# Gate copies and outputs of a state space stage two pairs later, a small store moved to GpSimd, and group norm sums placed ahead of the last attention tile

## The reference, cut to what matters

```python
y_attn = diff_attention(q, k, v, ...) @ w_attn_branch
xbc = silu(causal_depthwise_conv(xbc, conv_w, conv_b))          # 24 chunks of 128 channels
dt  = softplus(dt_raw + dt_bias);  a = -exp(a_log)
cum = cumsum(dt * a)                                            # per head, along the tokens
w[t, s] = (C_t . B_s) * exp(cum_t - cum_s) * dt_s   for s <= t  # per head, 32 heads
y   = w @ x_head + d_skip * x_head
y   = y * silu(z);  y = rms_norm of each of 4 groups of 512 channels
y_ssd = y @ w_ssd_branch
mixed = (sigmoid(g_attn) * y_attn + sigmoid(g_ssd) * y_ssd) @ w_out
```

## Time and profile before

| what | us |
|---|---|
| median of 3 runs | 1904.21 (1900.37 to 1904.4) |
| the profiled execution, its own time | 1904.04 |
| its span, first to last instruction | 1902.4 |
| TensorE busy | 1691.4 (89%) |
| VectorE busy | 917.0 (48%) |
| ScalarE busy | 556.3 (29%) |
| GpSimd busy | 326.9 (17%) |
| mean granted clock of TensorE | 0.968 of full speed |

### The profile page before, as it was taken

How to read it: one execution, slowest core, us unless ns; L and a number is a source line. 1 busy time by engine, 2 the same in 40 slices (tenths; PEclk the granted TensorE clock), 3 DMA queues, 4 the chain that set the end, 5 groups by cost and what they waited for, 6 DMA issues and landing times.

```text
span 1902.4 us, 30539 instructions
## 1 busy us (share of the span) xinstructions
PE 1691.4 (89%) x12330; PEld 1587.1 (83%) x12330; DVE 917.0 (48%) x2286; ACT 556.3 (29%) x1511; POOL 326.9 (17%) x300
## 2 busy tenths in 40 slices
PE   5999989989999878777898799867699999999998
PEld 4788868778879878776898799867599999989998
DVE  5641373444146666776797765458743210231200
ACT  0111223660033444433457321224623110132100
POOL 0100000000003444444424221224500000020000
PEclk9998999999999999999999999988899999999999
DMA  8962348323439999999999999999967888755783
GB/s 363 373 233 91 128 117 224 109 92 129 155 105 403 407 420 421 421 421 419 421 412 412 418 420 420 420 391 397 353 240 248 329 291 298 253 194 192 275 292 132
DMA packets 85450, 563.15 MB, mean 296 GB/s; under 512 B 8832, under 2 KB 17600, under 8 KB 17984
## 3 DMA queue, kind: packets, MB, share of 16 engines
q0 software_dynamic: 39744, 289.42, 37.1%
q1 hardware_dynamic: 38992, 256.05, 36.4%
q10 hardware_dynamic: 6576, 15.76, 3.1%
HBM read 556.96 MB, written 4.23 MB: 295 GB/s over the span
## 4 chain that ended last, share of the span: by engine, by line
PE 67%; DMA 19%; DVE 6%; ACT 4%; issue 3%; ACTq 0%; SPq 0%; POOL 0%; DVEq 0%
PE PS L885 30%; PE PS L633 21%; DMA AUX<-in_peer_uv_dram,SCR 10%; PE PS L849 7%; DMA ring<-in_stream_dram 6%; DMA CONV<-in_peer_uv_dram,SCR 1%; DMA V<-in_peer_uv_dram,SCR 1%; PE PS L704 1%; DVE PROJ L2048 1%; PE PS L655 1%; PE PS L679 1%; PE PS L753 1%; ACT PROJ L1401 1%; ACT small L1393 0%; PE PS L978 0%
## 5 line engine op out<-in xcount | busy, mean ns | idle before, releaser
L633 PE MATMUL PS<-H,ring 128*128 128x256 f32 x1280 | 292.8, 391 | 7.8 <-DMA ring<-in_stream_dram 4.1
L633 PEld LDWEIGHTS PS<-H,ring 128*128 128x128 f32 x1280 | 249.5, 197 | 45.0 <-issue 9.7
L849 PE MATMUL PS<-PROJ,AUX 128*128 128x128 f32 x1632 | 204.1, 284 | 71.5 <-ACT PROJ L1401 71.1
L885 PE MATMUL PS<-H,ring 128*128 128x128 f32 x2272 | 262.0, 276 | 3.9 <-DMA ring<-in_stream_dram 2.1
L885 PEld LDWEIGHTS PS<-H,ring 128*128 128x128 f32 x2272 | 258.3, 193 | 5.1 <-issue 4.1
L849 PEld LDWEIGHTS PS<-PROJ,AUX 128*128 128x128 f32 x1632 | 193.5, 197 | 80.1 <-ACT PROJ L1401 80.0
L1204 POOL DMA_INDIRECT AUX<-in_peer_uv_dram,SCR x124 | 148.5, 1197 | 473.5 <-DVE SCR L2032 228.7
L849 PE MATMUL PS<-PROJ,CONV 128*128 128x128 f32 x1328 | 173.1, 293 | 50.8 <-ACT PROJ L1401 50.8
L849 PEld LDWEIGHTS PS<-PROJ,CONV 128*128 128x128 f32 x1328 | 166.4, 207 | 56.1 <-ACT PROJ L1401 55.7
L885 PE MATMUL PS<-PROJ,ring 128*128 128x128 f32 x1664 | 192.5, 276 | 9.6 <-DMA ring<-in_stream_dram 9.6
L885 PEld LDWEIGHTS PS<-PROJ,ring 128*128 128x128 f32 x1664 | 188.9, 192 | 11.7 <-DMA ring<-in_stream_dram 9.9
(11 more groups left out here) (337 smaller groups left out, 1948.9 us busy)
## 6 DMA issues: line engine op xcount, KB each, us to landing
ring<-in_stream_dram SPq DMA_DIRECT2D x185, 1024.0 KB
AUX<-in_stream_dram SPq DMA_DIRECT2D x51, 1024.0 KB, 4.9
AUX<-in_ada_dram POOLq DMA_DIRECT2D x16, 1024.0 KB, 9.9
PROJ<-in_ada_dram ACTq DMA_DIRECT2D x4, 1024.0 KB, 20.3
AUX<-in_ada_dram SPq DMA_DIRECT2D x4, 1024.0 KB, 19.9
bias_skewed<-AUX ACTq DMA_DIRECT2D x1, 3072.0 KB, 34.2
ring<-in_stream_dram ACTq DMA_DIRECT2D x2, 1024.0 KB
PROJ<-in_rgw_dram ACTq DMA_DIRECT2D x2, 1024.0 KB, 10.4
```

The lines of the kernel that those rows point to most:

```text
L633: mm = pe.matmul(acc(n, c), w[:, k, c * P:(c + 1) * P], src[:, g * DC + k, :], start=(g == 0 and k == 0 and (c == 0 or groups == 1)), stop ...
L849: mm = pe.matmul(y_chunk(t, c), UV[b][:, D + c * P:D + (c + 1) * P], DIAG[turn % ND], start=(k == 0 and c % 4 == 0), stop=(k == SPT - 1), ...
L885: mm = pe.matmul(acc2(u, n)[:, c * P:(c + 1) * P], w[:, k, c * P:(c + 1) * P], src, start=(g == 0 and k == 0 and (c == 0 or groups == 1)), ...
```

## The change

- ScalarE copies gate tile (h + 2)/4 behind segment h and decay h-1, for h = 6, 10, ..., 26, instead of tile 1 + h/4 ahead of segment h, for h = 4, 8, ..., 24.
- VectorE runs `gate_out` two pairs behind the weighing instead of one.
- The store of the cumulative sums is issued by GpSimd instead of ScalarE, with a semaphore of its own.
- TensorE makes the four group norm sums ahead of the fourth attention tile instead of behind it. VectorE's work is put in matching order: two groups' squares are added behind each of the first two attention outputs, and groups 0 and 1 are normed before the fourth attention output is taken, groups 2 and 3 after it.
- Two semaphores of ScalarE are merged into one (`early_exp`).

```diff
-            for t in range(4):
+            for t in range(3):
                 project("attn", t, YA)
             for g in range(GROUPS):
                 pe.wait_ge(S("squares_added"), g + 1)
                 sum_chunks(("gn", g), CONV[:, 4 * g:4 * g + 1, :], 1)
+            project("attn", 3, YA)
...
-            pool.wait_ge(S("rows_stored"), 32)
+            wait_taken(pool, "cumt")
+            pool.dma_start(cum_rows, CUMT).then_inc(S("cumt_stored"), 16)
+            pool.wait_ge(S("cumt_stored"), 16)
             pool.wait_ge(S("conv_sum"), 24)
             load_rows(0)
...
                     taken(act.activation(CUMT, bank("cumt")[0:SSD_HEADS, 0:TOK], ACT.Copy), "cumt")
-                    wait_taken(act, "cumt")
-                    act.dma_start(cum_rows, CUMT).then_inc(S("rows_stored"), 16)
...
-            act.wait_ge(S("rows_stored"), 32)
+            act.wait_ge(S("rows_stored"), 16)
+            act.wait_ge(S("cumt_stored"), 16)
             for h in range(SSD_HEADS):
 
-                if h % 4 == 0 and 4 <= h <= 24:
-                    g_out(1 + h // 4)
                 segment(h)
                 if h:
                     decay(h - 1)
+                if h % 4 == 2 and 6 <= h <= 26:
+                    g_out((h + 2) // 4)
...
             for pair in range(SSD_HEADS // 2):
                 weigh(2 * pair)
                 weigh(2 * pair + 1)
-                if pair >= 1:
-                    gate_out(pair - 1)
+                if pair >= 2:
+                    gate_out(pair - 2)
+            gate_out(SSD_HEADS // 2 - 2)
             gate_out(SSD_HEADS // 2 - 1)
...
+            dve.wait_ge(S("g_ready"), 2)
+            attn_out(0)
+            add_squares(0)
+            add_squares(1)
+            attn_out(1)
+            add_squares(2)
+            add_squares(3)
+            attn_out(2)
+            group_norm(0)
+            group_norm(1)
+            attn_out(3)
+            group_norm(2)
+            group_norm(3)
+            dve.wait_ge(S("ys_ready"), 4 * GROUPS)
```

More of the change, by code:

```diff
@@ L1234, in _ @@
             act.wait_ge(S("params_landed"), 32)
-            act.activation(small[:, 240:248], pc("c", 0, 8), ACT.Silu).then_inc(S("c_ready"), 1)
+            act.activation(small[:, 240:248], pc("c", 0, 8), ACT.Silu).then_inc(S("early_exp"), 1)
             act.wait_ge(S("h_ready"), DC)
@@ L1239, in _ @@
             act.wait_ge(S("lam_dots"), 2)
-            act.activation(small[:, 18:20], small[:, 16:18], ACT.Exp).then_inc(S("lam_exp"), 1)
+            act.activation(small[:, 18:20], small[:, 16:18], ACT.Exp).then_inc(S("early_exp"), 1)
             def copy_out(name, t, dst):
@@ L1727, in _ @@
             dve.memset(EPS2_COL, EPS_2).then_inc(S("eps_set"), 1)
-            dve.wait_ge(S("c_ready"), 1)
+            dve.wait_ge(S("early_exp"), 1)
             ada_pair(0)
@@ L1815, in _ @@
                 if h == 0:
-                    dve.wait_ge(S("lam_exp"), 1)
+                    dve.wait_ge(S("early_exp"), 2)
                     did(dve.scalar_tensor_tensor(small[:, 20:21], small[:, 19:20], -LAMBDA_INIT, small[:, 18:19],
@@ L1909, in _, with attn_out @@
                 weigh(2 * pair + 1)
-                if pair >= 1:
-                    gate_out(pair - 1)
+                if pair >= 2:
+                    gate_out(pair - 2)
+            gate_out(SSD_HEADS // 2 - 2)
             gate_out(SSD_HEADS // 2 - 1)
-            dve.wait_ge(S("g_ready"), 2)
-            for t in range(4):
+            def attn_out(t):
                 n = colt("attn", t)
@@ L1920, in _, with add_squares @@
                     evacuated(dve.tensor_tensor(MIX[:, k, :], acc(n, c), G[:, k, :], ALU.mult), "attn", t)
-                dve.wait_ge(S("ys_square"), 4 * (t + 1))
-                a, b = CONV[:, 4 * t:4 * t + 2, :], CONV[:, 4 * t + 2:4 * t + 4, :]
+            def add_squares(g):
+                dve.wait_ge(S("ys_square"), 4 * (g + 1))
+                a, b = CONV[:, 4 * g:4 * g + 2, :], CONV[:, 4 * g + 2:4 * g + 4, :]
                 did(dve.tensor_tensor(a, a, b, ALU.add))
@@ L1925, in _, with group_norm @@
                 dve.tensor_tensor(a[:, 0, :], a[:, 0, :], a[:, 1, :], ALU.add).then_inc(S("squares_added"), 1)
-            for g in range(GROUPS):
+            def group_norm(g):
                 wait_taken(dve, ("gn", g))
@@ L1932, in _ @@
                         .then_inc(S("ys_ready"), 1)
-                dve.wait_ge(S("ys_ready"), 4 * (g + 1))
+            dve.wait_ge(S("g_ready"), 2)
[12 more added lines that the diff above has]
+            dve.wait_ge(S("ys_ready"), 4 * GROUPS)
             for t in range(4):
```

## The result

The changed kernel takes 1878.92 us (median of 4 runs, 1873.24 to 1882.81), before 1902.29 (4 runs, 1898.66 to 1904.4). The ratio is 0.9877, 95% interval 0.9839 to 0.9914: 23.4 us faster, with 16 to 31 in the interval. The same kernel timed again against 11 runs of before gave 0.9868 (0.9848 to 0.9887). The profiled execution took 1882.8 (span 1880.9), 21.2 less than that of before.

The account below looks back on a forecast made before the run. TensorE, holding 67% of the chain that ended last, was taken as the bound. Front 4.1, state space part 7.7 and norm sums 5.8 sum to 17.6 us; 1904.0 - 17.6 = 1886.4, stated as 1886, range 1879 to 1891.

Parts of the forecast that it names:

- the weights of gate tile 0: Front: SP's load shut out during the bias store, then delayed by a row load; weights land about 310.3, front gains 4.1.
- the row load's 2.5 us: Front: GpSimd's first 1 MB load, from about 300, takes 2.5 us of the DMA engines, so TensorE waits 2.5 us.
- Part 1: State space part: later gate copies and outputs two pairs late; turns 10.40 to 8.50, 10.6 won less 2.9 for clock, 7.7.
- the 10.6 + 0.7 forecast: Tail behind the last gate tile: 10.6 us, plus 0.7 lost on the last pair to the slower clock.
- Part 3: Group norm sums ahead of the last attention tile: 2.9 of time before the "ssd" tile plus 2.9 of slow clock, 5.8.
- clock term of 2.9: First "ssd" tile: the slow clock behind the old stall, 0.62 over 7.65 us, goes away, winning 2.9 us.
- Part 2's first half: Small store by GpSimd: TensorE wins 5.9 idle, 0.65 and 2.2 on two tiles, 8.8 up to gate tile 0.
- (a): Rival, front: gate tile 0's weights come in time, front 8.8 instead of 4.1, 1881.7 us; chance 0.21.
- Its first form: Rival, front: small store shut out by the bias store as SP's queue is; row load only at 305 or later; 8.8.
- (b): Rival: clock stays at its upper level, 2.4 GHz, in both new gaps; 2.2 + 2.9 more, 1881.3 us; chance 0.14.
- (c): Rival, front: ScalarE is held behind the bias store whatever follows, front gains nothing, 1890.5 us; chance 0.07.
- (d): Rival, state space part: late bank read ties the engines in a ring every pair, 35.1 slower there, 1929 us; chance 0.03.

Follow-up runs that it names:

- the one with sixteen transfers: Changed kernel with the bias store cut into 16 transfers of 8 positions; one run, 1910.99 us.
- changed twice: The changed kernel and its repeat without any edit, one profile each; 1878.92 us and 1878.36 us.
- store alone: Kernel before with only the small store of the cumulative sums moved from ScalarE to GpSimd; 1894.22 us, ratio 0.9956.
- one pair late: Changed kernel with the outputs taken one pair late again, gate tiles still copied out later; 1880.35 us, ratio 0.987 to before.
- spread: Changed kernel with the last five gate tiles ahead of pairs 2, 5, 8, 11, 14 and odd heads' decay ahead of the next segment; 1870.48 us.
- gate alone: Kernel before with only the gate tiles copied out later and the outputs taken two pairs late; 1894.45 us, ratio 0.9951.
- norm alone: Kernel before with only the group norm sums ahead of the last attention tile, VectorE's order matched; 1896.76 us, ratio 0.9976.
- the three with the bias store cut: Changed kernel with the bias store in 4 transfers, 16 transfers, or two of half the width; one run each, 1888.67, 1910.99 and 1889.3 us.

## Why the prediction was wrong, point by point

**The failed step is the weights of gate tile 0.** I wrote that q1 "moves nothing" while the bias store writes, took from it that the tile's data start when that store is over (304), and put the row load's 2.5 us on top and 2.2 us of slow clock. In the kernel after, TensorE ends the tile that frees the slot at 281.6, and SP issues the load then. The queues of that kernel from 292 to 294 and from 294 to 296 stand below that line:

```profile
281.75 0.33 SPq L591 DMA_DIRECT2D ring<-in_stream_dram  x1
```

```profile
q10 hardware_dynamic: 132, 0.20, 90.6%
...
q10 hardware_dynamic: 96, 0.15, 67.9%
q1 hardware_dynamic: 27, 0.22, 26.1%
```

Its data start at about 294, some 12 us behind the issue, with the bias store going on until 313.6 (it landed 41.9 us after its issue). Before, the issue was at 291.4 and the data began at 304.3, 13 us; over ten profiles (all but the one with sixteen transfers) it is 11.3 to 12.9. In five of them (changed twice, store alone, one pair late, spread) the bias store's last row moves 16 to 19 us after the tile's first data, which tells the two readings apart. The silence was a wait that runs from the issue, not a queue shut out until the store's end; the end of the store at 306.9 (34.2 us after its issue) only happened to lie near 291 + 13. That q1 "moves nothing" from 290 to 300 was true of the trace before; what did not follow was that it stays silent for as long as the store lasts. So the load moved forward with its issue, and the row load, issued at 299.46, came behind it and not ahead. The front won its upper end, 8.8 us. The store by GpSimd alone shows the same 8.76. I had the number that tells the two readings apart, the time of the issue, and had only looked at when the data began.

**A second, smaller miss:** the 2.17 us stall ahead of the transposes stays, as forecast, but the clock behind it does not fall, 1.29 us. The transposes took 3.9 us in all five profiles without a stall of TensorE at head 5 (changed twice, store alone, one pair late, spread), and 5.4 us in all six with one (before, gate alone, norm alone, and the three with the bias store cut, where ScalarE was held by its own issues). So the second fall goes with the first stall, 50 us earlier; how, is open.

**Part 1 was right.** Turns 8.60 for 8.50; the tail 380.23 to 391.64 = 11.4 us, for the 10.6 + 0.7 forecast; the clock fell in it, and cost 1.4 us on the attention tiles for the 2.2 forecast. My reason for the tail's bank wait (1.61 and 1.86 us ahead of the pairs) held. What I had not seen is that this half of the edit is not needed: with the outputs one pair late again, the later copies alone gave the short turns.

**Part 3 was right in its sum:** 6.2 us alone for 5.8. TensorE did not wait for the last chunks, where I had found 1 us of cover. Its clock term of 2.9 does not stand by itself, as the store by GpSimd alone shows (1.12 us won at full clock with the sums in their old place): it is won only because the new order also hides VectorE's scaling.

**Part 2's first half was right:** 8.8 us up to gate tile 0 is 5.9 + 0.65 + 2.2, and VectorE's convolution stayed hidden.

**The sum.** 17.6 forecast; 4.7 for the tile, 1.3 for the clock at the transposes and 0.3 for the rest (0.8 less in the state space part, 1.1 more behind it) give the 23.9 of the table. Of the rivals, (a) came true in its effect. Its first form did not: the small store landed 14.9 us after its issue. The second, no queue shut out by another, is near what happened, but I had no wait of 12 us in it. (b) did not come true: the clock fell in the tail. (c) and (d) did not. The 1.3 us lay outside all the ends from which I made the range.

That the time lies just outside the range is chance. As a gain, the measured 23.4 us lies inside the 13.3 to 25.2 that the range was made from. I had counted from 1904.0, and the runs of before in this comparison have a median of 1902.29, 1.7 us less; the 0.08 us by which the range is missed is far below the 9.6 us between the fastest and the slowest run of the changed kernel. The miss that the traces show is the front's, 4.1 forecast and 8.76 measured.

## What to carry to other kernels

When a transfer's data appear only as another big one ends, look at when it was issued before calling it blocked until then: a wait counted from the issue moves forward with the issue, a closed queue does not. When an engine's pace shows in a tail where another idles, move the idle engine's bulk work back among the small steps: five gate tiles placed every third pair instead of every second, with an earlier decay, were worth 8 us more. A wait taken off a loop should be tried in halves: here one of two edits made the loop short, and with the other TensorE's work came in fewer, wider spaced bursts and its clock fell.

## What the runs showed of the hardware

Beside a 3 MB store of 1536-byte rows (0.10 MB per us at 0.9 of the DMA engines), the next transfer from SP's queue moved its first data 11.3 to 12.9 us after its issue in ten profiles, with the same store in 4 transfers and with rows of half the size as well. A 32 KB store from GpSimd's queue moved its first data 6.7 to 13.9 us after its issue in seven (all but the one with sixteen transfers, where it was 2.3), and a 1 MB load from that queue, issued when SP's tiles were already moving beside the store, after 4.0 to 4.2 in five. A second transfer issued by ScalarE behind the store held ScalarE itself: 6.12 us for one, 8.06 for all four pieces of the store together, 28.21 for all sixteen; a copy or an activation behind the first alone was not held (272.46 in the profile after). Two heads of 64 outputs whose inputs are both ready take 0.70 us in TensorE together and 0.65 each if they come apart, so the same tail is less busy when its heads come in pairs: 6.01 of 8.20 us before, 4.76 of 9.60 in the changed kernel, and there the clock fell. But the clock does not follow such gaps one for one: behind the same 2.13 us of idle it was 0.62 before and 1.00 with the store by GpSimd alone.
